# RWKV sample state update: one stacked product per head pair and half, with part of its masked operand made by GpSimd

## What is computed

```
sa = einsum('bhvk,bhk->bhv', S, -kk_t)
S  = S * w_t + sa (x) (kk_t * a_t) + v_t (x) k_t
```

## Time and profile before

| | us |
|---|---|
| median of three timed runs | 1253.14 |
| the profiled execution, its own time | 1253.41 |
| its span (first to last instruction) | 1251.3 |
| PE busy | 1212.3 (97%) |
| DVE busy | 460.1 (37%) |
| ACT busy | 251.2 (20%) |
| POOL busy | 39.2 (3%) |

### The profile page before, as it was taken

How to read it: one execution, slowest core, us unless ns; L and a number is a source line. 1 busy time by engine, 2 the same in 40 slices (tenths; PEclk the granted TensorE clock), 3 DMA queues, 4 the chain that set the end, 5 groups by cost and what they waited for, 6 DMA issues and landing times.

```text
span 1251.3 us, 18361 instructions
## 1 busy us (share of the span) xinstructions
PE 1212.3 (97%) x7890; PEld 567.3 (45%) x7890; DVE 460.1 (37%) x958; ACT 251.2 (20%) x552; POOL 39.2 (3%) x93
## 2 busy tenths in 40 slices
PE   8999999999999999999999999999999999998997
PEld 5777776746433434344343434433333433343332
DVE  2357986754312331333233232332322323222234
ACT  2113432521311111111111111111111111111013
POOL 7000010000100000000000000000000000000000
PEclk9999999999999999999999999999999999999998
DMA  9732202485999999999999999999999999999995
GB/s 280 174 97 73 60 20 70 128 338 193 375 426 427 427 426 427 427 427 427 427 426 426 427 427 428 427 427 428 426 426 427 427 426 427 427 426 427 428 427 202
DMA packets 54843, 436.89 MB, mean 349 GB/s; under 512 B 9877, under 2 KB 25304, under 8 KB 30057
## 3 DMA queue, kind: packets, MB, share of 16 engines
q1 hardware_dynamic: 53634, 432.13, 84.0%
q0 software_dynamic: 1040, 3.54, 0.9%
q10 hardware_dynamic: 86, 0.02, 0.0%
HBM read 430.79 MB, written 4.89 MB: 348 GB/s over the span
## 4 chain that ended last, share of the span: by engine, by line
PE 74%; DMA 21%; DVE 3%; ACT 1%; issue 1%; SPq 0%; DVEq 0%; ACTq 0%
PE bank L1410 26%; DMA ring<-in_w_gate_up 16%; PE bank L1441 13%; PE bank L766 10%; PE bank L1386 6%; DMA mix<-in_w_down 5%; PE bank L1480 4%; PE bank L1201 3%; PE bank L1432 2%; PE bank L959 1%; PE bank L1471 1%; DVE mix L2237 1%; PE bank L793 1%; PE bank L1509 0%; PE bank L1458 0%
## 5 line engine op out<-in xcount | busy, mean ns | idle before, releaser
L1410 PE MATMUL bank<-ring,mix 128*64 128x512 f32 x1568 | 361.8, 600 | 17.6 <-DMA ring<-in_w_gate_up 14.4
L1410 PEld LDWEIGHTS bank<-ring,mix 128*64 128x64 f32 x1568 | 105.6, 137 | 229.2 <-issue 203.1
L1441 PE MATMUL bank<-ring,mix 128*64 128x512 f32 x736 | 167.8, 598 | 1.2 <-DMA ring<-in_w_down 1.1
L2595 DVE TENSOR_TENSOR hTb<-bank,w2a 128x512 f32<-128x512 f32 x32 | 22.1, 692 | 366.7 <-PE bank L1432 366.7
L766 PE MATMUL bank<-hTb,ring 128*128 128x320 f32 (+1 forms) x480 | 139.9, 445 | 1.4 <-issue 1.4
L1928 ACT ACTIVATE mix<-bank,nf 128x256 f32<-128x256 f32 x64 | 26.9, 471 | 426.3 <-PE bank L1386 426.2
L2647 DVE TENSOR_TENSOR mix<-mix,bank 128x512 f32<-128x512 f32 x70 | 48.2, 688 | 174.5 <-PE bank L1480 174.5
L1410 PE MATMUL bank<-mix 128*64 128x512 f32 x480 | 112.1, 599 | 0.0
L766 PEld LDWEIGHTS bank<-hTb,ring 128*128 128x128 f32 x480 | 89.9, 192 | 40.2 <-issue 4.5
L1441 PEld LDWEIGHTS bank<-ring,mix 128*64 128x64 f32 x736 | 49.8, 136 | 88.1 <-issue 84.9
L1441 PE MATMUL bank<-mix 128*64 128x512 f32 x288 | 65.8, 598 | 1.9 <-DMA mix<-in_w_down 1.9
(11 more groups left out here) (415 smaller groups left out, 1094.5 us busy)
## 6 DMA issues: line engine op xcount, KB each, us to landing
ring<-in_w_gate_up SPq DMA_DIRECT2D x98, 2048.0 KB, 28.2
ring<-in_w_down SPq DMA_DIRECT2D x46, 2048.0 KB, 30.7
mix<-in_w_gate_up SPq DMA_DIRECT2D x30, 2048.0 KB, 29.0
mix<-in_w_down SPq DMA_DIRECT2D x17, 2048.0 KB, 31.4
ring<-in_w_in SPq DMA_DIRECT2D x15, 1024.0 KB, 6.1
ring<-in_w_out SPq DMA_DIRECT2D x2, 2048.0 KB, 9.2
hx<-in_x_prompt SPq DMA_DIRECT2D x4, 512.0 KB, 3.9
out<-ring POOLq DMA_DIRECT2D x1, 2048.0 KB, 10.7
```

The costliest lines, as they stand in the source:

```text
L1410: last_ = mm(b_[64 * half:64 * half + 64, :], toks, w[:, o_:o_ + NCOL], start=(c == 0), stop=(c == KT - 1))
L1441: last_ = mm(b_[r:r + 64, :], lhs, w[:, o:o + NCOL], start=(j == 0 and q == 0), stop=(j == 1 and q == 3))
L2595: v.tensor_tensor(halves(gg), halves(banks[3][:, :]), bias(e, 0), ALU.add).then_inc(S("g1"), 1)
```

## The change

`send(j)` becomes two products with 128 rows of contraction instead of four with 64: for each half `p`, the weights are `b` of that head on partitions 0 to 63 and `k` on 64 to 127, and the moving operand has the masked `u` on 0 to 63 and the masked `v` on 64 to 127. For this

- `bks` goes to two banks, one for each `p`, with `b` on the lower and `k` on the upper half, and ScalarE copies it in two COPYs of 256 columns;
- masked `u` of `p = 0` stays with ScalarE (8 ACTIVATEs, now on 64 partitions); masked `u` of `p = 1` is made by VectorE (2 TENSOR_TENSORs of 64 x 1024, which take the place of the two of 128 x 1024); masked `v` of both halves is made by GpSimd (4 TENSOR_TENSORs of 64 x 1024), after `hsend` 7 is filled and ahead of the issue of the HGRN2 store;
- the banks of `bks`, `hsend` 4 to 7, `W`, `Ys`, `btok`, `ktok` and `bonus` are written out in the table.

```diff
-    add("bks")
-    add("hsend", 4)
-    add("W", 2)
-    add("Ys", ended=False)
-    add("btok", 2)
-    add("ktok", 2, ended=False)
+    add("bks", 2, (1, 2))
+    add("hsend", 4, (3, 4, 5, 0))
+    add("W", 2, (6, 7))
+    add("Ys", 1, (5,), ended=False)
+    add("btok", 2, (1, 2))
+    add("ktok", 2, (3, 4), ended=False)
...
-    add("bonus", 4, (4, 5, 0, 1))
+    add("bonus", 4, (4, 0, 5, 1))
...
+            pool.wait_ge(S("vtok_ready"), 3)
+            pool.wait_ge(S("unit_filled"), U("hsend", 8))
+            for x in range(2):
+                for p, o in ((0, uv0[64:128, 2 * x:2 * x + 2]), (1, uv1[x][64:128])):
+                    r = slice(64 * p, 64 * p + 64)
+                    ins = g.tensor_tensor(o, vtoks[r, 2 * x:2 * x + 2, :].unsqueeze(2).broadcast_to([64, 2, NS, RN]),
+                                          seqm[r, :].unsqueeze(1).unsqueeze(3).broadcast_to([64, 2, NS, RN]), ALU.mult)
             ins.then_inc(S("qm_ready"), 1)
             pool.wait_ge(S("hsend_ready"), 8)
...
-            b = free("bks", 0)
-            for s, src in enumerate((ra, rk)):
-                for j in range(4):
+            b = [free("bks", 0), free("bks", 1)]
+            for j in range(4):
+                for s, src in enumerate((ra, rk)):
                     for p in range(2):
-                        o = 256 * s + 64 * j
-                        last = mm(b[half(p), o:o + 64], src[half(p), j, NP_:NT], ident[half(p), half(p)], start=True, stop=True)
-            filled(last, "bks")
+                        last = mm(b[p][half(s), half(j)], src[half(p), j, NP_:NT], ident[half(p), half(p)], start=True, stop=True)
+                        if (j, s) == (3, 1):
+                            filled(last, "bks")
...
+                pe.wait_ge(S("qm_ready"), 4)
                 for p_ in range(2):
-                    mm(b_[half(p_), :], bks[half(p_), 0, j_, :], um[j_][half(p_)].rearrange("p b v -> p (b v)"), start=True, stop=False,
-                       skip_group_check=True)
-                for p_ in range(2):
-                    last_ = mm(b_[half(p_), :], bks[half(p_), 1, j_, :], vm[j_][half(p_)].rearrange("p b v -> p (b v)"), start=False,
-                               stop=True, skip_group_check=True)
+                    w_ = uv1[j_ // 2][:, j_ % 2] if p_ else uv0[:, j_]
+                    last_ = mm(b_[half(p_), :], bks[:, j_, p_, :], w_.rearrange("p b v -> p (b v)"), start=True, stop=True)
...
-            for x, o in enumerate((CBASE, K0)):
-                signal(v.tensor_tensor(at(o, 1024).rearrange("p (j b v) -> p j b v", j=2, b=NS),
-                                       vtoks[:, 2 * x:2 * x + 2, :].unsqueeze(2).broadcast_to([P, 2, NS, RN]),
-                                       seqm[:, :].unsqueeze(1).unsqueeze(3).broadcast_to([P, 2, NS, RN]), ALU.mult), "wr_ready")
+            for x in range(2):
+                signal(v.tensor_tensor(uv1[x][0:64], us[64:128, 2 * x:2 * x + 2, :].unsqueeze(2).broadcast_to([64, 2, NS, RN]),
+                                       seqm[64:128, :].unsqueeze(1).unsqueeze(3).broadcast_to([64, 2, NS, RN]), ALU.mult), "wr_ready")
```

More of the change, by code:

```diff
@@ L393, in build @@
         ktok = hTb[:, 1024:2048].rearrange("p (a d) -> p a d", d=512)
-        bks = lor[:, :, :].rearrange("p a t -> p (a t)")[:, 0:512].rearrange("p (s j v) -> p s j v", s=2, v=RN)
+        bks = lor[:, :, :].rearrange("p a t -> p (a t)")[:, 0:512].rearrange("p (j g v) -> p j g v", j=4, v=RN)
         us = at(K0 + 2 * W5, 256).rearrange("p (j t) -> p j t", t=64)
@@ L410, in build @@
         s0t = [t.rearrange("p (b j c v) -> p b j c v", b=2, j=4, c=2) for t in (mix[:, 3 * W5:3 * W5 + 1024], at(A0, 1024))]
-        um = [at(ITOK + 512 * j, 512).rearrange("p (b v) -> p b v", b=NS) for j in range(4)]
-        vm = [at(o, 512).rearrange("p (b v) -> p b v", b=NS) for o in (CBASE, CBASE + 512, K0, K0 + 512)]
+        uv0 = at(ITOK, 2048).rearrange("p (j b v) -> p j b v", j=4, b=NS)
+        uv1 = [at(o, 1024).rearrange("p (j b v) -> p j b v", j=2, b=NS) for o in (CBASE, K0)]
         sout = [t.rearrange("p (j k) -> p j k", j=4) for t in (mix[:, 0:512], mix[:, 512:1024], hTb[:, KT * NTP - 1024:KT * NTP - 512], hTb[:, KT * NTP - 512:KT * NTP])]
@@ L693, in _ @@
                 ins = g.tensor_copy(own_query(j), rr[:, j, NP_:NT].rearrange("p (q t) -> p q t", t=TS))
+            ins.then_inc(S("qm_ready"), 1)
+            pool.wait_ge(S("vtok_ready"), 3)
[5 more added lines that the diff above has]
+                                          seqm[r, :].unsqueeze(1).unsqueeze(3).broadcast_to([64, 2, NS, RN]), ALU.mult)
             ins.then_inc(S("qm_ready"), 1)
@@ L1860, in _ @@
                     ready(cp(o, b), "R0")
-            ready(cp(bks[:, :, :, :].rearrange("p s j v -> p (s j v)"), wait_filled("bks", 0)[:, :]), "bks")
+            for p in range(2):
+                ready(cp(bks[:, :, p, :], wait_filled("bks", p)[:, 0:256].rearrange("p (j v) -> p j v", v=RN)), "bks")
             act.wait_ge(S("unit_filled"), U("hsend", 8))
@@ L1864, in _ @@
             for b_ in range(NS):
-                a(at(ITOK, 2048).rearrange("p (j b v) -> p j b v", j=4, b=NS)[:, :, b_, :], us[:, :, :], ACT.Copy,
-                  scale=seqm[:, b_:b_ + 1])
+                a(uv0[0:64, :, b_, :], us[0:64, :, :], ACT.Copy, scale=seqm[0:64, b_:b_ + 1])
             for stage, dst in (("btok", btok), ("ktok", ktok)):
@@ L2380, in _ @@
             take_w(4)
-            dve.wait_ge(S("vtok_ready"), 3)
+            dve.wait_ge(S("Us_ready"), 1)
             dve.wait_ge(S("unit_filled"), U("R0", 2))
-            for x, o in enumerate((CBASE, K0)):
-                signal(v.tensor_tensor(at(o, 1024).rearrange("p (j b v) -> p j b v", j=2, b=NS),
-                                       vtoks[:, 2 * x:2 * x + 2, :].unsqueeze(2).broadcast_to([P, 2, NS, RN]),
-                                       seqm[:, :].unsqueeze(1).unsqueeze(3).broadcast_to([P, 2, NS, RN]), ALU.mult), "wr_ready")
+            for x in range(2):
+                signal(v.tensor_tensor(uv1[x][0:64], us[64:128, 2 * x:2 * x + 2, :].unsqueeze(2).broadcast_to([64, 2, NS, RN]),
+                                       seqm[64:128, :].unsqueeze(1).unsqueeze(3).broadcast_to([64, 2, NS, RN]), ALU.mult), "wr_ready")
             dve.wait_ge(S("router_in"), 48)
```

## The result

The changed kernel takes 1261.78 us in the median of four runs (1261.49 to 1264.8), the kernel before 1253.35 (1250.74 to 1253.98): a ratio of 1.0075, with a 95% interval of 1.0061 to 1.0090. The forecast was 1258.1 with a range to 1261.5. The sign and the first mechanism, VectorE held up by GpSimd, were right; the time lies outside the range. The profiled execution took 1261.74 us, its span is 1259.6, 8.3 more than before.

The account below looks back on a forecast made before the run. The weight stream bounds the experts, its start set by TensorE; +7.5 us to `C` and -2.55 to the chain give +4.95, a forecast of 1258.1 us, own range 1256 to 1260.5, 8 in 10 range 1250.8 to 1261.5.

Parts of the forecast that it names:

- The end follows TensorE one for one: A microsecond TensorE gains or loses between 225 and 253 us moves the end equally, unless another engine becomes late.
- `C` waits for the `UX` copy: `C` on TensorE starts 0.49 us after VectorE's `UX` copy, so time added to VectorE there is TensorE's at once.
- `send`, -2.55 from `C` to the chain: Four shorter `send` save 0.86 us each, 3.44 in all; 2.55 of it is kept from `C` to the chain.
- the 0.9 us that VectorE was to cost at `centered`: TensorE waits at `centered` for VectorE's `sent(2)`, until 9.2 us after `C` instead of 8.3, losing 0.9 us.
- `bks`, 0: `bks` may be up to 0.5 us shorter, hidden behind ScalarE's `atok` copies: value 0, between -0.1 and +0.2.
- `hsend` 7, +0.65: `hsend` 7 waits for ScalarE to read the second `R0` unit's bank: +0.65 us for TensorE, masked `u` and GpSimd.
- Masked `v`, 2.35 us each: GpSimd's four TENSOR_TENSORs of 1024 elements take 2.35 us each, 9.4 in all, from about 229.65.
- VectorE blocked, +7.5 at `C`: VectorE's nine two-operand instructions wait for GpSimd: 0.15 us and three whole instructions, 7.05; `C` starts 7.5 us later.
- TensorE has nothing ahead of `C` to fill this with: While `C` is delayed by 7.5 us, TensorE has no other work and stands idle for 6 to 7 us.
- The store moves behind the four and is hidden: The HGRN2 store moves from 230.75 to about 241.9, the loads behind it later; hidden unless 10 us later still.
- +4.95: The forecast's sum: +7.5 us to the start of `C`, -2.55 from there to the chain.
- Rival 2: VectorE keeps GpSimd out until about 237.6; `send(0)` waits 4.0 us, the sum is +1.4, 1254.5 us; chance 0.08.

Follow-up runs that it names:

- e5: e1 with other banks: `hsend` 7 on bank 7, `W` on banks 6 and 0; 1254.80 us.
- e8: e5 with the `x` reloads and expert pieces 0 to 3 held until the second `centered` product, and VectorE's four gate products spread between its waits; 1253.20 us.
- e1: The changed kernel with GpSimd's four masked products moved earlier, two at 210 us and two at 225; 1255.82 us.
- e2: The changed kernel with GpSimd's four masked products replaced in place by five MEMSETs, which read nothing, the `v` term left out; 1260.40 us.
- e9: The changed kernel with only VectorE's order changed: `UX` copies right behind the two masked `u`, decays, router weights and gate products later; 1257.38 us.
- e3: The changed kernel with five more products, their result unused, on TensorE before it waits for `UX`; 1260.13 us.
- e7: The kernel before with only the HGRN2 store issued later, at 238.59 instead of 230.75; 1255.95 us.
- e10: e9 with `x` reloads and expert pieces 0 to 3 held until the second `centered` product, and the `w_out` load until `Y0` is filled; 1257.34 us.
- e11: e8 with the `w_out` load issued only when `Y0` is filled; 1250.62 us, ratio 0.9973 to 0.9991 to the kernel before.

## Why the prediction was wrong, step by step

One more row of the kernel before, inside `send(0)`, which runs from 240.93 to 242.65:

```profile
241.80 0.33 PE L1294 MATMUL bank<-ring,hTb 64*64 64x64 f32 x4
```

- **The end follows TensorE one for one**: right, 7.86 us at the output projection and at piece 4, 8.3 in the span.
- **`C` waits for the `UX` copy**: nearly. Before, TensorE's own `bonus` products (L1150, 236.65 + 2.42 = 239.07) ended as late, so the first 0.1 us or so of VectorE's loss cost nothing: 4.66 us lost there, 4.51 at `C`.
- **`send`, -2.55 from `C` to the chain**: near, by two errors that cancel. By itself it is -2.36. A new `send` takes 252.19 to 253.19 = 1.00 us to the next product, not 0.86, and the 3.44 us counted 1.72 for each old one, although products of the next stage ran inside it (the row above). In the new kernel none do, and `Q` behind a `send` takes 1.10 us instead of 0.93. Against this, the 0.9 us that VectorE was to cost at `centered` is not there: e5 and e8 have no wait before it.
- **`bks`, 0**: right. It took 0.65 us instead of 1.10, and TensorE then waited 0.67 for the `atok` copies.
- **`hsend` 7, +0.65**: right. The four took 2.71 us instead of 2.17; e5 takes the wait away again.
- **Masked `v`, 2.35 us each**: too long. Unblocked it is 1.90. The line through the two small rows (128 and 8 elements) overstated the cost for an element at 1024. Whether half the partitions matter no run shows.
- **VectorE blocked, +7.5 at `C`**: mechanism right, size off. The sum had the rest of the first GpSimd instruction and three whole ones. At 1.90 us the first had ended (231.58) when VectorE came at 232.05, so it was the rest of the second and two more: 4.66 us of block, +5.14 at `C` with `hsend`. e1, e2 and e9 show the mechanism by time, by kind of instruction and by order.
- **"TensorE has nothing ahead of `C` to fill this with"**: true, and I stopped there. An idle TensorE loses its clock, at 2.56 us in this timeline, a term that the sum did not have. e3 shows the cause of the half clock; it does not show that the time falls by so much without it.
- **The store moves behind the four and is hidden**: the failed step. As a transfer it was hidden: its readers came later still. But its traffic stood over TensorE's instruction fetch: +1.31 us, and the next wait, in the chain, came while the loads that had moved with it ran: +1.41. That these loads caused it is argued from the times alone; in e3 this wait is 0.21 with the store moved as well. e7 and e10 show a wait behind the store without the loads.

In short, the prediction had -2.55 from `C` to the chain and nothing in the chain; measured are 15.25 - 13.74 = +1.51 and +1.23. With the sizes measured the step from +4.95 would have been +5.14 - 2.36 = +2.78, 1255.9 us; the two terms that I had not got, half clock and instruction fetch, add 2.56 + 1.31 + 1.23 = 5.10. My errors of size, 2.2 us too much together, covered part of what was missing, and even so the time fell outside. None of the rivals named either term. Rival 2 (VectorE keeps GpSimd out) is refuted by the turns the two engines take.

**What stays open.** What decides when a fetch packet gets through is not shown; only the times are. It is not simply the end of the store: in e7, with the store running from 241 to about 249, a packet starts between 246.25 and 246.5, and before the change one started near 235, two microseconds into the store. Nor is it known when a packet was asked for. Issue waits differ from one execution to the next: e5 ran from 1251.7 to 1259.1, e10's profile (1253.71) is the fastest of its five, so the stalls of one profile need not be those of the median. The changed kernel's profiled execution (1261.74) lies at its median.

## What to carry to other kernels

Before work goes to GpSimd, list VectorE's two-operand SBUF instructions in that window, and price each meeting at a whole GpSimd instruction; put the GpSimd work where VectorE reads PSUM or waits, or put what TensorE waits for ahead of the blocked ones. When an idle gap of TensorE grows by some microseconds, look in the trace for a gap of that length and what the granted clock did behind it, and price it. When a bulk transfer moves, ask also what TensorE's instruction fetch was doing in that time: in straight-line code with many small products a transfer of 8 us can show up as an "issue" wait.

## What the runs showed of the hardware

- Instruction fetch of TensorE is not always hidden. In this stretch of small products the 16 KB packets start 3.25 and 3.75 us apart when the DMA queues are quiet (e11). Beside the store, at 275 GB/s, none started from 239.9 to 246.4 us in e10, and beside the loads, at 300 GB/s in the mean, none from 244 to 253.4 in e1; TensorE waited 2.85 and 4.82 us. Over all kernels with a wait at all, single waits were 0.2 to 4.8 us. The Trainium skill says that the sequencer fetches 16 KiB blocks over its own DMA queue while it executes the current one, at a cost mostly hidden (Runtime: NRT & Kernel Launch, Instruction fetch mechanics). The trace agrees on the size and on a queue of its own; the cost was hidden in the kernel before but for 0.18 us, and not in e7, where only the store had moved.
- The lower clock level outlasts the idle time that brought it: with TensorE idle from 239.7 to 244.1 the granted clock was 1.00 up to 243, 0.51 in the next microsecond, and 0.50 up to 249, with TensorE busy again. A wait for instructions can cost it in the same way: 0.73 in the mean of 250 to 253 us in e3, behind 3.15 us, and 0.68 in e9, behind 2.85. It need not: in e10, behind the same 2.85 us, it is 1.00 in that stretch.
- A GpSimd TENSOR_TENSOR of 1024 elements on 64 partitions takes 1.90 us, with broadcast operands; a MEMSET of 2048 takes 5.52 / 3 = 1.84 us, and VectorE beside it was not held up.
